# Which products are split in two, when a bias mask is added, and the order of two weight roundings, in a three-layer f32 transformer kernel on one core

## What is computed

```python
# first block, layers 0 and 1
h = h + mla_stick_breaking_mixer(rms_norm(h, g_mix[0]), ...)   # layer 0: x @ w_in, heads, @ w_out
h = h + swiglu(rms_norm(h, g_ffn[0]), w_gate[0], w_up[0], w_down[0])
h = h + chunk_band_mixer(rms_norm(h, g_mix[1]), w_qkv, rel_bias, w_out)  # layer 1
h = h + swiglu(rms_norm(h, g_ffn[1]), w_gate[1], w_up[1], w_down[1])
x = rms_norm(h, g_final)
# second block, on concat([meta, x])
proj = rms_norm_2(stream, mix_norm_g) @ w_in        # convolution, attention and gate columns
stream = stream + (g_a * y_a + g_b * y_b) @ w_merge_out
up = causal_depthwise_conv(rms_norm_2(stream, ffn_norm_g) @ ffn_up, ffn_dw_w, ffn_dw_b)
a, b = split(up);  stream = stream + (silu(a) * b) @ ffn_down
out = rms_norm_2(stream, final_norm_g)[:, 16:]

def swiglu(u, w_gate, w_up, w_down):
    return (silu(u @ w_gate) * (u @ w_up)) @ w_down
```

## Time and profile before

| | us |
|---|---|
| median of 3 runs | 1073.23 |
| the runs | 1074.32, 1071.95, 1073.23 |
| profiled execution | 1074.75 |
| its span, first to last instruction | 1073.0 |
| TensorE busy | 1056.7 (98% of the span) |
| VectorE busy | 754.6 |
| ScalarE busy | 576.0 |
| GpSimd busy | 207.5 |

### The profile page before, as it was taken

One profiled execution on the slowest core, in us unless ns is written; L12 is line 12 of the kernel. 1 busy time (PEld: TensorE's weight loads), 2 busy tenths in 40 slices (PEclk: granted clock), 3 DMA queues, 4 the chain that ended last, 5 costly groups with the idle time before them and its releaser, 6 DMA issues.

```text
span 1073.0 us, 22189 instructions
## 1 busy us (share of the span) xinstructions
PE 1056.7 (98%) x8777; PEld 1024.1 (95%) x8777; DVE 754.6 (70%) x1238; ACT 576.0 (54%) x853; POOL 207.5 (19%) x189
## 2 busy tenths in 40 slices
PE   9999999999999999999999999999999999999997
PEld 8998899999999889999999999999899999999997
DVE  6778665555757776655655589987988668887652
ACT  5668554444545555644455454446668355565532
POOL 0432030000210000300000287885450000000000
PEclk9999999999999999999999999999999999999999
DMA  9735356656675443566545745553335535654451
GB/s 278 218 111 173 104 188 190 191 169 213 222 239 176 139 157 96 184 194 195 176 159 197 234 121 172 153 184 118 115 123 166 185 123 190 196 187 149 163 173 40
DMA packets 187940, 181.31 MB, mean 169 GB/s; under 512 B 17951, under 2 KB 186284, under 8 KB 187867
## 3 DMA queue, kind: packets, MB, share of 16 engines
q1 hardware_dynamic: 187179, 177.94, 52.4%
q0 software_dynamic: 544, 2.10, 0.7%
q10 hardware_dynamic: 144, 0.26, 0.1%
HBM read 179.24 MB, written 1.05 MB: 168 GB/s over the span
## 4 chain that ended last, share of the span: by engine, by line
PE 88%; DVE 6%; ACT 4%; issue 2%; POOL 1%; DVEq 0%; ACTq 0%
PE ps L575 27%; PE ps L576 27%; PE ps L580 27%; DVE w_lo L397 2%; ACT w_hi L381 1%; DVE ps L2716 1%; PE ps L1882 1%; PE ps L2056 1%; PE ps L2249 1%; PE ps L2065 1%; POOL w_lo L409 1%; PE ps L1851 0%; PE ps L1803 0%; PE ps L1875 0%; PE ps L1863 0%
## 5 line engine op out<-in xcount | busy, mean ns | idle before, releaser
L397 DVE TENSOR_TENSOR w_lo<-raw,w_hi 128x2048 fp32r<-128x2048 f32 (+3 forms) x157 | 333.3, 2137 | 138.9 <-ACT w_hi L381 138.7
L381 ACT ACTIVATE w_hi<-raw 128x2048 fp32r<-128x2048 f32 (+3 forms) x182 | 316.5, 1754 | 32.1 <-PE ps L580 22.1
L575 PE MATMUL ps<-u_hi,w_hi 128*128 128x256 f32 x944 | 264.8, 281 | 0.4 <-DVE w_lo L2437 0.4
L576 PE MATMUL ps<-u_lo,w_hi 128*128 128x256 f32 x944 | 261.4, 277 | 0.0
L580 PE MATMUL ps<-u_hi,w_lo 128*128 128x256 f32 x940 | 260.3, 277 | 0.0
L575 PE MATMUL ps<-m_hi,w_hi 128*128 128x258 f32 (+2 forms) x792 | 227.2, 287 | 1.2 <-POOL w_lo L409 0.5
L576 PE MATMUL ps<-m_lo,w_hi 128*128 128x258 f32 (+2 forms) x792 | 223.7, 282 | 0.0
L580 PE MATMUL ps<-m_hi,w_lo 128*128 128x258 f32 (+2 forms) x792 | 223.7, 282 | 0.0
L575 PEld LDWEIGHTS ps<-u_hi,w_hi 128*128 128x128 f32 x944 | 177.7, 188 | 3.0 <-issue 1.9
L576 PEld LDWEIGHTS ps<-u_lo,w_hi 128*128 128x128 f32 x944 | 177.3, 188 | 0.2
L580 PEld LDWEIGHTS ps<-u_hi,w_lo 128*128 128x128 f32 x940 | 176.6, 188 | 0.0
(11 more groups left out here) (368 smaller groups left out, 1617.8 us busy)
## 6 DMA issues: line engine op xcount, KB each, us to landing
raw<-in_w_in SPq DMA_DIRECT2D x24, 1024.0 KB, 5.4
raw<-in_w_gate SPq DMA_DIRECT2D x22, 1024.0 KB, 5.3
raw<-in_w_up SPq DMA_DIRECT2D x22, 1024.0 KB, 5.4
raw<-in_ffn_up SPq DMA_DIRECT2D x22, 1024.0 KB, 5.1
raw<-in_w_down SPq DMA_DIRECT2D x16, 768.0 KB, 4.7
raw<-in_od_w_qkv SPq DMA_DIRECT2D x12, 1024.0 KB, 5.2
raw<-in_w_down SPq DMA_DIRECT2D x16, 640.0 KB, 4.9
raw<-in_ev_w_in SPq DMA_DIRECT2D x7, 1024.0 KB, 10.5
```

The lines of the kernel that those rows point to most:

```text
L381: nc.scalar.activation(w_hi[t % RING][:, 0:n], raw[t % RAW][:, 0:n], ACT.Copy).then_inc(hi_done, 1)
L397: nc.vector.tensor_tensor(w_lo[t % RING][:, 0:n], raw[t % RAW][:, 0:n], w_hi[t % RING][:, 0:n].bitcast(F32), ALU.subtract).then_inc(lo_don ...
L575: nc.tensor.matmul(out_ap, a_h, b_h, start=start and n == 0, stop=False)
L576: nc.tensor.matmul(out_ap, a_h, b_l, start=False, stop=False)
```

## The change

Three things. First, `product` and its callers can halve any triple's third product instead of the last one, and the places are others: the first triple of the given tile, `halved=0`. They are unit 1 (first tile) and unit 7 (second tile, second triple) of `ph_in`, unit 3 of `ph_out0` and of `ph_out1`, units 1 (first tile) and 2 (second tile, behind `late_sums`) of `ph_ffn0` and `ph_ffn1`, unit 1 of the loop body of `ph_down0` and `ph_down1` (so executed twice each), unit 1 of `ph_qkv`, and units 1, 5, 7, 11 and 15 of `ph_down2`. Executed, these are 18 halved products where there were 4. Second, GpSimd's mask adds wait until VectorE has written `w_lo` of unit 4 of `ph_down0`, instead of the second `u_lo` of the next layer. Third, ScalarE rounds unit 2 of the mixer in four pieces between the first four `m_hi`, and unit 3 ahead of the table load and the first two evictions. The diff, with `out0_group` and `out1_group` passing `halved` on left out:

```diff
@@ -570,17 +570,18 @@
-    def product(out_ap, pairs, start=True, stop=True, halved=False):
+    def product(out_ap, pairs, start=True, stop=True, halved=None):
         for n, (a_h, a_l, b_h, b_l) in enumerate(pairs):
             nc.tensor.matmul(out_ap, a_h, b_h, start=start and n == 0, stop=False)
             nc.tensor.matmul(out_ap, a_h, b_l, start=False, stop=False)
             last = n == len(pairs) - 1
-            if halved and last:
-                return halves(out_ap, a_l, b_h, stop)
+            if n == halved:
+                mm = halves(out_ap, a_l, b_h, stop and last)
+                continue
             mm = nc.tensor.matmul(out_ap, a_l, b_h, start=False, stop=stop and last)
         return mm
@@ -608,16 +609,16 @@
-            feature_tile(outs[0], s, KT, UC, 0, xh, xl, halved=halved)
+            feature_tile(outs[0], s, KT, UC, 0, xh, xl, halved=0 if 0 in fresh else None)
             if between is not None:
                 between()
-            mm = feature_tile(outs[1], s, KT, UC, P, xh, xl)
+            mm = feature_tile(outs[1], s, KT, UC, P, xh, xl, halved=0 if 1 in fresh else None)
@@ -636,7 +637,8 @@
             mm = feature_tile(ps[:, 2 * p + t, 0:T1], s, nk, UC, t * P, lambda kt: a_hi[:, kt, :],
-                              lambda kt: a_lo[:, kt, :], x0=k0, start=k % 4 == 0, stop=k % 4 == 3)
+                              lambda kt: a_lo[:, kt, :], x0=k0, start=k % 4 == 0, stop=k % 4 == 3,
+                              halved=0 if t == 0 and k in FRESH_DOWN[name] else None)
@@ -973,6 +975,7 @@
+    FRESH_DOWN = {"ffn0": (1,), "ffn1": (1,), "ffn2": (1, 5, 7, 11, 15)}
@@ -1029,7 +1032,7 @@
             two_tiles(ph, i, k, n, u_h(n), u_l(n), name if k == 0 else None,
                       (lambda: late_sums(name)) if late and k == 2 else None,
-                      late and k in (1, 3))
+                      {1: (0,), 2: (1,)}.get(k, ()) if late else ())
@@ -1257,7 +1260,7 @@
         pool.wait_ge(sem("bias_landed"), 32)
-        pool.wait_ge(sem("xl_done"), split_at["mix1"] + 2)
+        pool.wait_ge(lo_done, ph_down0.u0 + 5)
@@ -1569,7 +1572,18 @@
         both_roots()
-        norm_round_act(norm_at["mix2"][1], KT, T2, u_h(T2))
+        t, turns = ph_mix.u0 + AHEAD, KT // 2
+        act.wait_ge(raw_landed[t % RAW], landed[t])
+        wait(act, unit_done, t - (RING - 1))
+        part = widths[t] // turns
+        for kt in range(KT):
+            act.wait_ge(sem("un_done"), norm_at["mix2"][1] + kt + 1)
+            nc.scalar.activation(u_h(T2)(kt), work[:, kt, 0:T2], ACT.Copy).then_inc(sem("xh_done"), 1)
+            if kt < turns:
+                cols = slice(kt * part, (kt + 1) * part)
+                a = nc.scalar.activation(w_hi[t % RING][:, cols], raw[t % RAW][:, cols], ACT.Copy)
+                if kt == turns - 1:
+                    a.then_inc(hi_done, 1)
         plain_root()
@@ -1678,9 +1692,11 @@
         for x in range(MIX_END + 1):
+            if x == MIX_STARTS[1]:
+                split_hi(ph_mix, 0, 1)
             for T in TILES_AT.get(x, ()):
                 mix_evicted(T)
-            if x - 1 in MIX_STARTS:
+            if x - 1 in MIX_STARTS[2:]:
                 split_hi(ph_mix, 0, MIX_STARTS.index(x - 1))
@@ -1953,7 +1969,7 @@
-                    mm = product(fm_bank(k, t), [terms], kt == 0, kt == KT - 1)
+                    mm = product(fm_bank(k, t), [terms], kt == 0, kt == KT - 1, 0 if (k, t, kt) in ((1, 0, 0), (7, 1, 1)) else None)
@@ -2042,7 +2058,7 @@
             for kt in OUT0_ORDER:
-                mm = out0_group(3, kt, t)
+                mm = out0_group(3, kt, t, 0 if t == 0 and kt == OUT0_ORDER[0] else None)
@@ -2109,7 +2125,7 @@
-                        mm = product(out[:, t, :], [terms], kt == 0, kt == KT - 1)
+                        mm = product(out[:, t, :], [terms], kt == 0, kt == KT - 1, 0 if (k, t, kt) == (1, 0, 0) else None)
@@ -2158,7 +2174,7 @@
             for kt in range(KT):
-                mm = out1_group(3, kt, t)
+                mm = out1_group(3, kt, t, 0 if t == kt == 0 else None)
```

More of the change, by code:

```diff
@@ L577, in product, with feature_tile @@
             last = n == len(pairs) - 1
-            if halved and last:
-                return halves(out_ap, a_l, b_h, stop)
+            if n == halved:
+                mm = halves(out_ap, a_l, b_h, stop and last)
+                continue
             mm = nc.tensor.matmul(out_ap, a_l, b_h, start=False, stop=stop and last)
         return mm
-    def feature_tile(out_ap, s, nk, n, col, xh, xl, x0=0, start=True, stop=True, halved=False):
+    def feature_tile(out_ap, s, nk, n, col, xh, xl, x0=0, start=True, stop=True, halved=None):
         hi, lo = pw(w_hi[s], nk, n), pw(w_lo[s], nk, n)
@@ L609, in by_tokens, with two_tiles @@
         mm.then_inc(unit_done, 1)
-    def two_tiles(ph, i, k, n, xh, xl, ready=None, between=None, halved=False):
+    def two_tiles(ph, i, k, n, xh, xl, ready=None, between=None, fresh=()):
         s, p = begin_unit(ph, i, k)
@@ L2002, in _, with out0_group @@
             mm.then_inc(unit_done, 1)
-        def out0_group(k, kt, t):
+        def out0_group(k, kt, t, halved=None):
             s = (ph_out0.u0 + k) % RING
@@ L2007, in out0_group @@
             return product(fm_bank(13 + k, t), [(hi[:, kt, cols], lo[:, kt, cols], o_hi[:, kt, :], o_lo[:, lo_tile(kt), :])],
-                           kt == OUT0_ORDER[0], kt == OUT0_ORDER[-1])
+                           kt == OUT0_ORDER[0], kt == OUT0_ORDER[-1], halved)
         def out0_part(k, j, t, x=None):
@@ L2121, in _, with out1_group @@
                 mm.then_inc(sem("tok_turned"), 1)
-        def out1_group(k, kt, t):
+        def out1_group(k, kt, t, halved=None):
             s = (ph_out1.u0 + k) % RING
@@ L2127, in out1_group @@
             return product(out1_bank(k, t), [(hi[:, kt, cols], lo[:, kt, cols], o3_hi[:, kt, :], o3_lo[:, kt, :])],
-                           kt == 0, kt == KT - 1)
+                           kt == 0, kt == KT - 1, halved)
         pairs_read_after = [ph_qkv.used_after[n] for n in range(3)]
```

## The result

| | us |
|---|---|
| before, median of 22 runs | 1073.02 (1071.62 to 1074.58) |
| after, median of 22 runs | 1073.62 (1072.29 to 1079.18) |
| ratio after to before | 1.0018, 95% interval 1.0011 to 1.0026 |
| profiled execution of after | 1072.90, span 1071.0 |

The forecast was 1070.9, faster by 2.3 us; measured is 0.6 us or 0.18% slower, within the 0.2% that the prediction counts as no change, and just outside its range (1073.6). The times of after fall into two groups: 14 of 22 lie from 1072.29 to 1074.12, median 1073.05, and 8 from 1077.14 to 1079.18, median 1077.8. Before has no time near 1077. The profiled execution belongs to the lower one, so the trace can't show the upper one.

The account below looks back on a forecast made before the run. TensorE was taken to bound the kernel, through product pace and waits. Terms 1.16 + 2.19 - 0.27 - 0.13 + 0.1 + 0.36 - 1.05 = 2.36 us saved, from median 1073.23 to 1070.9; range 1068.8 to 1073.6.

Parts of the forecast that it names:

- What bounds the kernel: Whole kernel: TensorE busy 1056.7 of 1073.0 us, so time leaves only through faster product spacing or fewer TensorE waits.
- the base of the sum: Whole kernel: 2.36 us saved, taken from the three-run median 1073.23 instead of the profiled 1074.75, giving 1070.9.
- Rival 3: Whole kernel: the median has less slow pace than the profile; lacking 1.2 us of it gives 1072.1; chance 0.08.
- 0.95 (the other terms, with both costs of 0.27): Halved products: feed-forward entries +1.16, both middle down projections -0.27 each, qkv -0.13, input projections +0.1, last down projection +0.36.
- The term of 1.64 behind the wait at 276: First down projection and next phase: without the wait, 372 products stay fast, each 4.4 ns shorter, saving 1.64 us.
- Entries, down projections, last projection: Halved products: two feed-forward entries save 0.58 each, second down projection costs 0.27, last down projection saves 0.36.
- Cover: 1.1 us: First down projection, unit 6 weights: remainder done near 274.6, TensorE needs it at 275.7, so the 0.82 wait goes.
- Mixer, -1.05: Mixer unit 0: GpSimd's pieces beside VectorE's m_lo cost 1.7 us, the vanished wait near 631 returns 0.67.
- Rival 1: Mixer: GpSimd's pieces cost nothing as VectorE is back first at every handover; gain 4.1 at most, 1069.1; chance 0.20.
- Fast staying fast is my assumption: Halved products in fast stretches: no row shows their effect; pace assumed to stay fast, each costing 0.13 us.
- Rival 4: Both feed-forwards: a halved product turns whatever pace it meets, leaving loops slow; about 1079; chance 0.10.
- The estimate of 2.7: Mixer: net loss bound if VectorE loses four whole GpSimd pieces of 0.9 us, by the skill's "whole instruction" rule.

Follow-up runs that it names:

- held_and_few_third: Changed kernel with GpSimd's mixer unit 2 pieces held until the eighth m_lo is written and 13 halved products removed, third run: median 1070.32 us, ratio 0.9985.
- mixer_alone: The kernel before with only the change's earlier rounding of the two mixer weight units: median 1074.16 us, ratio 1.0019.
- second_repair: Kernel of held_and_few_third plus one more halved product in unit 3 of each of the two feed-forwards: median 1070.06 us, ratio 0.9980.
- twelve_later: Kernel of held_and_few_third with the halved product behind the late sums moved from first to fifth triple of its tile: median 1070.00 us, ratio 0.9980.
- pieces_held: Changed kernel where GpSimd starts the four pieces of mixer unit 2 only when the eighth m_lo is written: median 1070.73 us, ratio 0.9986.

## Why the prediction was wrong

**What bounds the kernel: right.** TensorE's products and waits account for the differences between the traces, and fast and slow are 113.3 and 117.7 ns in every trace.

**The step that failed first is the base of the sum**, "from the median the sum gives 1070.9". The sum was made of slow stretches and waits of one execution that was 1.5 above the median, then taken off the median. Rival 3 named this and got 0.08. In the medians the parts brought 0.67 for the masks where the sum had 2.46 (0.82 + 1.64), 0.17 for all the halved products where it had 0.95 (the other terms, with both costs of 0.27), and -1.78 for the mixer where it had -1.05. The term of 1.64 behind the wait at 276 was a draw, there in two of four traces; that accounts for some 0.8 of what the masks lack, and the rest is open.

**Entries, down projections, last projection: mechanism right, net nearly nothing.** By the traces +0.6 and +0.3 for two times 0.58, +0.4 for 0.36, -0.25 for -0.27. In the medians all 18 halved products gave 0.17 us, and taking 13 of them out gave 0.8 to 0.9.

**"Cover: 1.1 us"**: the mechanism was right (u_lo stands until the mask add ends, the evictions do not), the size was wrong. The DMA landed later than assumed, so the add ended at 272.35 and not at 271.6, and TensorE, sped up by the change's own first part, wanted the weights 0.6 us sooner: 0.2 was left. It held in the trace of after; in held_and_few_third it did not.

**Mixer, -1.05: the mis-sized term.** The mechanism was right (GpSimd's four pieces beside VectorE's chain). The chain lost 2.1 where 1.7 was worked out, of which 0.2 is the slack that wasn't there, and gave back 0.78 where 0.67 was: 1.33 in the trace. In medians it was 1.78, with an interval of 1.1 to 3.0 (mixer_alone's ratio), so the trace's 1.33 is not refuted by it. I had no term for the fallen clock, 1.3 to 1.5 us in about one execution in six; in mixer_alone one of 11 has it, so it does not explain that median. Rival 1 (the pieces cost nothing) is refuted: with the pieces held back the same instructions take 0.47 again.

**"Fast staying fast is my assumption": right,** in all 57 halved products with a row of fast products just ahead of them. To count a repair close behind a disturbance as certain was an error (87 of 89). Rival 4 had the right place (a feed-forward's loop, over 4 us each) and the wrong rule: no fast stretch was turned by a halved product, and what likely happened is that a repair failed now and then. It was priced as all or nothing, so its part in the median, 1073.62 against 1073.05 for the lower group, had no place in the forecast. These 0.6 us are what carried the median from inside the stated range to its edge.

The Trainium skill, *SBUF — State Buffer*, section "Who interferes with whom", calls the port pair that VectorE and GpSimd share an exclusive lock, which whoever issues first holds for its whole instruction. The rows agree: the first u_lo stood until the end of the 4.06 us mask add, and VectorE's 0.47 became 0.96 beside pieces of 0.92, one piece for each instruction. The estimate of 2.7 made from it is twice the measured 1.33: by the rows the engines take turns, VectorE's own work of about 0.47 counts inside each 0.96, so four pieces cost four times 0.5 and not four times 0.9.

## What to carry to other kernels

Before you price what a stretch costs, look at whether it is slow in every execution: a trace with a time 1.5 us above the median can hold slow stretches that the median lacks, and a saving of 1.6 us was half gone for that. When you start another engine's work sooner, keep it out of the chain that feeds TensorE: here one wait on GpSimd made 0.5 us of gain out of 1.3 to 1.8 of loss. A repair that is put close behind a disturbance to gain 0.2 us failed 2 times in 89, and a stretch left slow without one cost 6.3 us; second_repair and twelve_later, 2.2 and 2.4 us faster than the kernel before (ratio 0.9980, interval 0.9972 to 0.9989 for both), repair later or twice.

## What the runs showed of the hardware

- Pace is drawn at a disturbance. The same wait left 371 products fast in two traces and slow in two, gaps that met fast pace left it slow 13 times in 35, late sums left the loop slow in 8 of 12 executions (by their times), and a gap longer by 0.07 us (0.18 for 0.11) was enough.
- A product split into two of 128 columns costs 0.11 to 0.13 us and was followed by fast pace 212 times in 214.
- TensorE's granted clock can fall from 2.4 to 1.2 GHz for 3.4 us in the middle of the kernel, after 3 us in which TensorE was busy for half. The trace of after has the same 1.5 of 3 us (12 products in 616 to 619) and no fall.
- ScalarE's table load and two evictions (1.28 and 0.69 us) came 0.67 us too late for TensorE with both weight roundings (2.85 us) ahead of them; with the 1.90 us one alone, in pieces_held, TensorE has no wait there.
- A VectorE instruction with both operands in SBUF took 0.96 us beside each GpSimd piece where it takes 0.47 alone.
